# Multiplying the recurrent outputs later on VectorE, in the mixer of a one-layer decoder step

## The reference

```
u = x * (1.0 + scale1) + shift1
p = u @ w_in                                   # cb, cc, cv | q, f, i, g
o, s = _gla_chunked(qh, kh, vh, log_f, s0)      # the recurrence, float32
o = o * rsqrt(mean(o * o) + RMS_EPS)
o = o * gnorm_w * silu(g)                       # the product that is moved
```

## Time and profile before

| | us |
|---|---|
| median of 3 runs (1986.83 to 1986.95) | 1986.94 |
| the profiled execution, its own time | 1986.83 |
| its span in the trace | 1985.2 |
| PE busy | 1783.3 (90%) |
| DVE busy | 1118.7 (56%) |
| ACT busy | 612.6 (31%) |
| POOL busy | 569.4 (29%) |

### The profile page before, as it was taken

How to read it: one execution, slowest core, us unless ns; L and a number is a source line. 1 busy time by engine, 2 the same in 40 slices (tenths; PEclk the granted TensorE clock), 3 DMA queues, 4 the chain that set the end, 5 groups by cost and what they waited for, 6 DMA issues and landing times. The chain is left out here.

```text
span 1985.2 us, 28737 instructions
## 1 busy us (share of the span) xinstructions
PE 1783.3 (90%) x9032; PEld 1378.5 (69%) x9033; DVE 1118.7 (56%) x1715; ACT 612.6 (31%) x746; POOL 569.4 (29%) x685
## 2 busy tenths in 40 slices
PE   5699999999999999999689995449999999999674
PEld 2388888888888899999478884126666676666331
DVE  3366666666666666555477665404456333455198
ACT  0433332333333322221211110105465433455142
POOL 0111112122222222202154443532344322334155
PEclk8899999999999999999799997659999999999897
DMA  9733333333333232231755443637899875797495
GB/s 333 219 91 96 96 96 88 89 95 96 96 95 87 84 87 79 77 98 39 240 180 159 150 137 128 213 102 249 290 341 360 286 233 169 233 324 289 192 380 190
DMA packets 295019, 341.88 MB, mean 172 GB/s; under 512 B 18631, under 2 KB 244424, under 8 KB 292476
## 3 DMA queue, kind: packets, MB, share of 16 engines
q1 hardware_dynamic: 271820, 283.37, 44.2%
q0 software_dynamic: 18000, 55.87, 7.7%
q10 hardware_dynamic: 5106, 1.42, 0.4%
HBM read 276.08 MB, written 64.55 MB: 172 GB/s over the span
## 5 line engine op out<-in xcount | busy, mean ns | idle before, releaser
L1401 DVE TENSOR_TENSOR w_gu_lo<-w_gu_raw,w_gu_hi (+1 forms) x64 | 146.4, 2291 | 144.8 <-ACT w_gu_hi L1394 144.6
L826 DVE TENSOR_TENSOR w_lo<-w_raw,w_hi 128x1024 fp32r<-128x1024 f32 x112 | 140.5, 1257 | 108.0 <-ACT w_hi L524 104.3
L626 POOL TENSOR_TENSOR o_r<-o_ms,neg_half 128x4 f32<-128x4 f32 (+1 forms) x16 | 16.8, 1050 | 639.4 <-DVEq L862 639.4
L678 PE MATMUL pr<-ub_hi,w_hi 128*128 128x288 f32 (+1 forms) x672 | 188.5, 334 | 0.0
L1909 PE MATMUL ph<-w_gu_hi,x_hi 128*128 (+1 forms) x408 | 177.0, 434 | 10.5 <-DVE x_lo L1866 10.4
L1932 PE MATMUL py<-w_dn_w,hhT 128*128 x400 | 184.8, 605 | 1.7 <-ACT hhT L1843 1.2
L678 PE MATMUL pr<-ub_hi,w_lo 128*128 128x288 f32 (+1 forms) x672 | 184.1, 328 | 0.0
L678 PE MATMUL pr<-ub_lo,w_hi 128*128 128x288 f32 (+1 forms) x672 | 183.6, 327 | 0.0
L678 PE MATMUL pr<-ua_hi,w_hi 128*128 128x512 f32 x448 | 181.8, 406 | 0.0
L678 PE MATMUL pr<-ua_hi,w_lo 128*128 128x512 f32 x448 | 176.9, 395 | 0.0
L678 PE MATMUL pr<-ua_lo,w_hi 128*128 128x512 f32 x448 | 176.9, 395 | 0.0
(11 more groups left out here) (338 smaller groups left out, 3391.8 us busy)
## 6 DMA issues: line engine op xcount, KB each, us to landing
w_raw<-in_w_in SPq DMA_DIRECT2D x112, 512.0 KB, 4.1
w_gu_raw<-in_w_e_gate SPq DMA_DIRECT2D x32, 1024.0 KB, 7.6
w_gu_raw<-in_w_e_up SPq DMA_DIRECT2D x32, 1024.0 KB, 11.3
w_dn_w<-in_w_e_down SPq DMA_DIRECT2D x32, 1024.0 KB, 8.7
w_ring<-in_w_mod SPq DMA_DIRECT2D x10, 2048.0 KB, 19.8
y_t<-y_scratch SPq DMA_DIRECT2D x16, 1024.0 KB, 7.3
x_cols<-in_x_prompt SPq DMA_DIRECT2D x32, 256.0 KB, 4.7
y_raw<-y_scratch SPq DMA_DIRECT2D x16, 512.0 KB, 4.9
```

The lines of the kernel that those rows point to most:

```text
L626: pool.tensor_tensor(o_r[:, 0:c], o_ms[:, 0:c], keep["neg_half"][:, 0:c], ALU.pow).then_inc(o_rs, 1)
L678: last = pe.matmul(pr[n % 2][:, a * 512:a * 512 + c], w[:, n % WS, k, :], x[:, k, a * c:(a + 1) * c], start=(k == 0 and m == 0), stop=(k = ...
L826: dve.tensor_tensor(w_lo[:, n % WS], w_raw[:, n % WRAW], w_hi[:, n % WS].bitcast(F32), ALU.subtract).then_inc(lo_done, 1)
L1401: dve.tensor_tensor(w_slot(keep["gu_lo"], s, lo, hi), w_slot(keep["gu_raw"], r, lo, hi), w_slot(keep["gu_hi"], s, lo, hi).bitcast(F32), AL ...
```

## The change

`recurrent_out(u - 1)` leaves the loop over the levels of ql, where it stood behind the second level (l == 1), and goes behind `split_lo(n + 4)`, ahead of the second `low_u` and of `split_lo(n + 5)`. Nothing else is altered; PE, ACT, POOL and SP have the same instructions in the same order.

```diff
                         dve.tensor_tensor(dst[:, :, 1, :], src[:, :, 1, :], wleft, ALU.mult)
                         dve.tensor_copy(dst[:, :, 0, :], src[:, :, 0, :])
                         dve.drain().then_inc(q_lev, 1)
-                        if l == 1 and u:
-                            recurrent_out(u - 1)
...
                     if u < FIRST_S:
                         low_u(q)
                     split_lo(n + 4)
+                    if u:
+                        recurrent_out(u - 1)
                     if u < FIRST_S:
                         low_u(q + 1)
                     split_lo(n + 5)
```

## The result

The changed kernel takes 2065.28 us (median of 4 runs, 2064.24 to 2067.18) against 1986.95 us (4 runs, 1986.83 to 1987.84): slower by 78.3 us, ratio 1.0394, 95% interval 1.0377 to 1.0412. A second set of runs gave 2068.43 against 1988.19 us, ratio 1.0406 (1.0389 to 1.0424).

The account below looks back on a forecast made before the run. PE's order alone was taken to bound the mixer. To 1986.9 us were added 57 us of standstill and 19 us of clock, 76 in all, giving 2063 us; its own range 2052 to 2076, the 8-in-10 range 2043 to 2082.

Parts of the forecast that it names:

- What bounds the kernel: Mixer: PE, busy 852.75 of 853.00 us at clock 1.00, alone sets the time; any stop is paid in full.
- Where L891 ends: Unit 6: L891 ends at 416.62, transposes start at 416.77, PE stands still 3.95 us; 57 us over fifteen units.
- 0.83 us brought forward: Unit 6 on DVE: taking L891 and its drain from the levels starts everything behind 0.83 us sooner.
- 1.7 us to spare: Unit 6 before the change: L891 ends at 411.14, transposes of v start at 412.82, so the product had 1.7 us slack.
- What waits behind the wait: Behind L703: PE's rest shifts as one; ACT's gg, SP's store and the earlier levels of ql cost nothing.
- The clock: Behind PE's stops in the mixer: granted clock falls in nearly every unit, 1.25 us each, 19 us; bounds 0 to 47.
- four fifths of the priced stretch: Clock term per unit: 1.25 us of the 1.6 us priced for one low stretch, part lying in the standstill.
- The page's rule: Skill page: each turn's idle gap makes the warm-up paid again; by it standstill and clock cost some 76 us.
- The clock holds: Rival for the mixer: only the standstill is paid, 1986.9 + 57 = 2044 us; 12 in 100.
- The clock stays low longer: Rival behind the stops: clock low for two stretches each time, 1986.9 + 57 + 47 = 2091 us; 8 in 100.
- PE goes on past the wait: Rival at L703: PE runs projection 3 meanwhile, 1986.9 us, half cover 2004; 3 in 100 for both.
- a few us either way: Later stages: same work in the same order, but the clock may fall at other instants, shifting time a few us.

Follow-up runs that it names:

- the other bank: Changed kernel with the transposed outputs written to PSUM tensor po in place of pt, product still late: 1988.13 us, ratio 0.9996 to the kernel before.
- the filled kernel: Changed kernel plus 16 unread 512-column matmuls (12 in units 13 to 15) on PE ahead of the transposes of v: 2045.88 us, ratio 1.0282.
- the second profile of the changed kernel: Profile from running the changed kernel again with no edit; that set measured 2068.43 us, ratio 1.0406 to the kernel before.
- half filled: Changed kernel plus only 8 unread matmuls (6 in units 13 to 15) ahead of the transposes of v: 2048.23 us, ratio 1.0301.

## Why the prediction was right, and where its size was off

- *What bounds the kernel.* Right. The mixer's growth is PE's standstill plus PE's slower matmuls (plus the filling, where there is one), in every kernel of the table to 0.6 us.
- *Where L891 ends.* Right. 3.95 us was worked out for unit 6 and 3.87 measured, 4.63 for unit 2 against 4.55, 2.8 for unit 15 against 2.77. In unit 6 most of the difference is in the term "0.83 us brought forward": from L969 to L826 it was 9.46 us (406.16 to 415.62) and is 8.56 now (439.02 to 447.58), so 0.90. Release and spacing came out as counted, 0.15 and 1.14 us. Sum 57 forecast, 55.2 measured; of the 1.7 us between them 0.8 are in units 7 (4.3 against 3.93) and 14 (3.2 against 2.81), for which no reason is shown. The "1.7 us to spare" left out the 0.15 us of the release: it is 1.5 us, as the product behind the fourth level shows.
- *What waits behind the wait.* Right. PE has no other new wait in the mixer, and gg and the store cost nothing. In the other bank the product is as late as in the changed kernel and the time is that of before. SP still issues a weight load and then the store (timeline of SP, unit 6, for the earlier trace rows), but the store's slack is gone: it goes out 0.07 us after the product's end at 449.40.

```profile
448.83 0.37 SPq L452 DMA_DIRECT2D w_raw<-in_w_in  x1
449.47 0.34 SPq L472 DMA_DIRECT2D y_scratch<-y_rec  x1
```

- *The clock.* The mechanism is right, shown by filling the stop: the wait and the fall go together, and 19 to 23 us with them. The size was low. 19 us were forecast from 1.25 us per unit; the two profiles have 25.9 and 26.3. The mis-sized term is "four fifths of the priced stretch", taken once per stop: I had one stretch per stop, priced at 1.6 us, and gave the second only as a rival of 8 in 100. The first profile has 19 stretches behind 13 stops, 64.9 us at the half level, of which 8.0 lie inside the stops. Fifteen single ones with the same 8.0 us hidden would have cost 19.7 us: the four fifths were near enough, and the second stretch behind 6 of the stops, less the 2 stops without one, is what was missing. The rival's "15 times two" and my "15 times one" are the two ends of what is a mix.
- *The page's rule.* The Trainium skill ("TensorE: Matmul & The Clock Gate", "HAM oscillation — how this bites in real kernels") has the warm-up paid anew in each turn that holds an idle gap. The runs agree nearly in full for the changed kernel's stops of 2.8 to 4.6 us (13 of 15) and in full for those of 3.9 to 6.3 us (15 of 15), and only in part for shorter ones (7 of 15 at 1.6 to 2.9 us), among which the gap of the earlier trace rows belongs.
- *Rivals.* "The clock holds" (2044 us) is ruled out by the granted clock; the filled kernel, in which it does hold, takes 2045.9 us. "The clock stays low longer" (2091 us) is ruled out by the time, but 6 of the 15 stops do what it says. "PE goes on past the wait" is ruled out by the rows of unit 6: no matmul of projection 3 starts between 445.44 and 449.55.
- *The total.* 2063 forecast, 2065.3 measured. That it came so near is in part luck. In the mixer the standstill was 2 us too high and the clock 7 us too low, 81 us in place of 76; outside the mixer the second profile of the changed kernel (2065.74 us) is 2.9 us shorter than the kernel before, where the forecast had only "a few us either way".
- *Sums in the working.* Twice 1.6 us x 15 is 48, not 47. 1986.9 + 15 x 1.1 is 2003, not 2004. Halfway from the forecast of 2063 up to 2091 is 2077, and the range went to 2082; the result lies inside either.

No kernel beats the one before. None was to be had from these edits, since the mixer's PE was without a gap; the other bank only shows that the early place isn't needed if `pt` is relieved.

## What to carry to other kernels

When one engine is busy without a gap, ask of each step on the others what the full engine waits for in it and how much later it may come: here 1.5 us of delay on a PSUM bank were free, and each us beyond was paid fifteen times. When the engine that stops is PE, price the clock behind the stop apart from the stop; at stops near 4 us it added 40 to 50%. Where a buffer's reader must move, look for a second buffer that is idle at that time, as `po` was.

## What the runs showed of the hardware

- The granted clock fell behind none of 15 stops of 0.9 to 2.1 us (product behind level 6), behind 3 of 15 of 1.4 to 2.7 us (half filled), 7 of 15 of 1.6 to 2.9 us, 7 of 15 of 1.7 to 3.4 us, 13 of 15 of 2.8 to 4.6 us in each of two profiles, and 15 of 15 of 3.9 to 6.3 us. Behind one of two equal stops it may fall and behind the other hold, and it may hold behind a longer stop where it falls behind a shorter one: in the second profile of the changed kernel it held behind unit 1's stop of 3.9 us. With the stops in the profiles of all kernels of the table put together by length, it fell behind none of 28 stops of 0.5 to 2.0 us, 18 of 37 of 2.0 to 3.0 us, 25 of 27 of 3.0 to 4.0 us and all 15 longer ones. In a forecast that is a share, not a threshold.
- The fall comes at times within the stop and at times up to 1.2 us after work has begun again, and it ends under dense matmuls.
- The kernel before itself ran between 1985.29 and 1992.69 us in 19 runs on one chip, where the four beside the first result lay within 1.0 us. Differences below 0.2% were left uncalled here for that reason; where in the program they arise was not looked for.
